# Down projections of an encoder trunk: twelve rows by seven products instead of eight, through a ring of units

## The reference, cut to what matters

```
def swiglu(h, w_gu, w_down):
    u = h @ w_gu
    return (silu(u[..., :D_FF]) * u[..., D_FF:]) @ w_down      # [512, 2816] @ [2816, 1024]

h = h + rmsnorm(swiglu(rmsnorm(h, ffn_pre[l]), ffn_w_gu[l], ffn_w_down[l]), ffn_post[l])    # l = 0, 1
kv = rmsnorm(h, kv_norm) @ w_kv                                # between the two layers
q = rmsnorm(h, mix_pre[1]) @ w_q
```

## Time and profile before

| | |
|---|---|
| median of 3 runs | 1087.94 us |
| the profiled execution's own time | 1087.81 us |
| its span | 1086.0 us |
| TensorE matmul busy | 1076.0 us (99%) |
| VectorE busy | 850.5 us (78%) |
| ScalarE busy | 589.0 us (54%) |
| POOL busy | 27.4 us (3%) |
| granted TensorE clock | 0.999 |

### The profile page before, as it was taken

The page is one execution under the profiler, slowest core; times in us unless marked ns, Lnnn a source line. Parts: engine busy times, 40 slices in busy tenths (PEclk is TensorE's granted clock), DMA queues, the critical chain, the costliest instruction groups (busy, mean ns, idle before and its releaser), DMA issues.

```text
span 1086.0 us, 17578 instructions
## 1 busy us (share of the span) xinstructions
PE 1076.0 (99%) x6925; PEld 967.5 (89%) x6925; DVE 850.5 (78%) x1165; ACT 589.0 (54%) x1013; POOL 27.4 (3%) x40
## 2 busy tenths in 40 slices
PE   8999999999999999999999999999999999999998
PEld 7887787889999999988889888889999999998886
DVE  5878986788888888889857798558988888869834
ACT  6377474565555555556435686555555555555523
POOL 2000000000000000000241000000000000000000
PEclk9999999999999999999999999999999999999999
DMA  6332233332333343251562201141244334341311
GB/s 207 104 102 69 78 108 117 96 98 79 98 116 93 104 117 103 93 194 75 138 175 71 48 1 40 40 117 53 84 118 117 91 105 117 108 151 54 136 58 78
DMA packets 150963, 107.24 MB, mean 99 GB/s; under 512 B 23921, under 2 KB 140769, under 8 KB 150882
## 3 DMA queue, kind: packets, MB, share of 16 engines
q1 hardware_dynamic: 150880, 106.12, 32.3%
q10 hardware_dynamic: 2, 0.00, 0.0%
HBM read 104.01 MB, written 2.10 MB: 98 GB/s over the span
## 4 chain that ended last, share of the span: by engine, by line
PE 96%; ACT 1%; DVE 1%; DMA 1%; issue 0%; DVEq 0%; ACTq 0%
PE ps L2214 12%; PE ps L2212 12%; PE ps L2210 12%; PE ps L1895 8%; PE ps L1896 8%; PE ps L1897 8%; PE ps L1915 8%; PE ps L1917 7%; PE ps L1921 7%; PE ps L1960 2%; PE ps L1962 2%; PE ps L1958 2%; PE ps L2141 1%; PE ps L1928 1%; PE ps L2315 1%; PE ps L2342 1%
## 5 line engine op out<-in xcount | busy, mean ns | idle before, releaser
L2210 PE MATMUL ps<-t_hi,w_hi 128*128 128x256 f32 x608 | 172.1, 283 | 0.0
L2212 PE MATMUL ps<-t_lo,w_hi 128*128 128x256 f32 x608 | 172.1, 283 | 0.0
L2214 PE MATMUL ps<-t_hi,w_lo 128*128 128x256 f32 x608 | 172.1, 283 | 0.0
L1269 DVE TENSOR_TENSOR w_lo<-raw,w_hi 128x1024 fp32r<-128x1024 f32 x81 | 102.1, 1264 | 74.7 <-ACT w_hi L743 74.6
L1895 PE MATMUL ps<-x_hi,w_hi 128*128 128x512 f32 (+1 forms) x384 | 137.5, 358 | 0.0
L1896 PE MATMUL ps<-x_lo,w_hi 128*128 128x512 f32 (+1 forms) x384 | 135.1, 352 | 0.0
L1897 PE MATMUL ps<-x_hi,w_lo 128*128 128x512 f32 (+1 forms) x384 | 135.1, 352 | 0.0
L2214 PE MATMUL ps<-x_hi,w_lo 128*128 128x256 f32 x456 | 129.0, 283 | 0.0
L2212 PE MATMUL ps<-x_lo,w_hi 128*128 128x256 f32 x456 | 129.0, 283 | 0.0
L2210 PE MATMUL ps<-x_hi,w_hi 128*128 128x256 f32 x456 | 129.0, 283 | 0.0
L743 ACT CAST w_hi<-raw 128x1024 fp32r<-128x1024 f32 x82 | 85.4, 1047 | 80.0 <-PE ps L1921 61.5
(11 more groups left out here) (286 smaller groups left out, 2445.9 us busy)
## 6 DMA issues: line engine op xcount, KB each, us to landing
raw<-in_ffn_w_gu SPq DMA_DIRECT2D x88, 512.0 KB, 4.6
raw<-in_ffn_w_down SPq DMA_DIRECT2D x36, 512.0 KB, 4.0
raw<-in_a_w_in SPq DMA_DIRECT2D x24, 512.0 KB, 3.9
raw<-in_a_w_out SPq DMA_DIRECT2D x12, 512.0 KB, 3.5
xr<-in_ffn_w_down SPq DMA_DIRECT2D x8, 512.0 KB, 7.6
raw<-in_b_w_o SPq DMA_DIRECT2D x16, 256.0 KB, 4.0
raw_q<-in_b_w_q SPq DMA_DIRECT2D x12, 256.0 KB, 4.6
h<-in_x SPq DMA_DIRECT2D x4, 512.0 KB, 5.5
```

Of the source, the lines that this page charges most:

```text
L1269: v.tensor_tensor(lo, raw_of(t), hi.bitcast(F32), ALU.subtract).then_inc(w_lo_ready, 1)
L2210: nc.tensor.matmul(ps[:, b, 0:HS], w_hi[:, slot, cols], hi, start=start, stop=False, skip_group_check=True)
L2212: nc.tensor.matmul(ps[:, b, 0:HS], w_hi[:, slot, cols], lo, start=False, stop=False, skip_group_check=True)
L2214: ins = nc.tensor.matmul(ps[:, b, 0:HS], w_lo[:, slot, cols], hi, start=False, stop=j == DC // 2 - 1, skip_group_check=True)
```

## The change: what it does

- The chunk takes twelve rows (4 to 15) instead of eight; the sevenfold scheme stays, each quarter now being six rows deep. Ten rows are plain instead of fourteen.
- Each phase is cut in three units of two rows. Splits, weight sums T1 to T4, matmuls and semaphores go unit by unit (`unit_done` in place of `phase_done`); the token sums S1 to S4 are one instruction each, now 1536 columns.
- The high and low parts of the weights go through a ring: units 0 and 1 of phases 1, 6, 7 and 4 in `x_hi`, their unit 2 in `w_hi` and `w_lo` place 0; phases 2, 3 and 5 in places 1 to 3. Phase 4 runs its units in the order 2, 0, 1.
- The raw weights lie in `raw` (rows 4 to 7), `work` (8, 9), `xr` (10 to 13) and `hr`, in the space of `hid` rows 0 to 3 (14, 15). Rows 8 and 9 are loaded between rows 5 and 6.
- The split of row 16 waits for unit 2 of phase 4; those of rows 17 to 19 for the units of phase 5.
- On VectorE fix_c22 stands before the split of row 16, and fix_c12, fix_c22 follow each other. keep_5 keeps its place on ScalarE.
- The own query tiles are issued later: Q6, Q7 and Q2 behind rows 19, 20 and 21, Q3 behind Q0, Q4 and Q5 behind Q1; each waits for phase 4. POOL scales Q6, Q7, Q2, K, Q0, Q3, V, Q1, Q4, Q5.

```diff
-OWN_LOADS = {15: 6, 16: 7, 17: 2, 18: 3, 19: 4, 20: 5}
+OWN_LOADS = {19: 6, 20: 7, 21: 2}
-C0, CP = 4, 4
+C0, CP = 4, 6
+UNITS = [(q, u) for q in PHASES for u in ((2, 0, 1) if q == 4 else (0, 1, 2))]
...
+        def chunk_b_hi(q, u):
+            if PHASES.index(q) % 2 == 0 and u < 2:
+                return x_hi[:, 4 * u:4 * u + 2, :]
+            return pair_of_weights(w_hi, 1 + u if PHASES.index(q) % 2 else 0)
...
+                def chunk_row(k):
+                    p = k - C0 - 4
+                    if p == 0:
+                        sp.wait_ge(lo_4, SEVEN * (f + 1))
+                    elif p == 2:
+                        sp.wait_ge(p3_done, SEVEN * (f + 1))
+                    elif p == 6:
+                        sp.wait_ge(hidlo_ready, plain_row(f, C0 - 1) + 1)
+                    sp.dma_start(chunk_raw(k), dn_v[f][k]).then_inc(chunk_landed[p], 16)
...
             def load_own_queries(m):
-                if m < 6:
-                    sp.wait_ge(hidlo_ready, plain_row(0, 2 * HID_RING - 1) + 1)
-                else:
+                sp.wait_ge(unit_done, unit(0, 4))
+                if m >= 6:
                     sp.wait_ge(fixes_done, fixed(0, "X"))
...
             load_queries(0)
+            load_own_queries(3)
             chunks(T_V, kv_v[:, :, 1, :])
             load_queries(1)
+            load_own_queries(4)
+            load_own_queries(5)
...
                 elif t >= 4 and chunk_place(t - 4) is not None:
-                    if t % 4 < 2:
-                        act.wait_ge(p7_done_half, 2 * chunk_of(t) + 2)
-                    else:
-                        act.wait_ge(phase_done, finished(chunk_of(t), 5))
+                    f, i = chunk_of(t), t % 4
+                    act.wait_ge(unit_done, unit(f, 4, 2) if i == 0 else unit(f, 5, i - 1))
...
+                chunk_high(5)
+                for t in range(2):
+                    keep_7(t)
+                chunk_high(4)
                 k = C0 + CK
                 split_hi(T_DN[f] + k)
...
+                chunk_low(7)
+                chunk_low(5)
+                chunk_low(4)
                 fix_c12()
+                fix_c22()
                 k = C0 + CK
                 split_lo(T_DN[f] + k)
                 hid_low(k)
                 split_lo(T_DN[f] + k + 1)
-                fix_c22()
                 hid_low(k + 1)
                 fix_c21()
...
+                def unit_by_unit(q):
+                    for at in UNITS:
+                        if at[0] == q:
+                            unit_ready(*at)
+                            for p in range(2):
+                                one(*at, p, 0)
+                                ins = one(*at, p, 1)
+                            ins.then_inc(unit_done, 1)
...
+                for u in range(3):
+                    unit_ready(7, u)
+                    one(7, u, 0, 0)
+                    ins = one(7, u, 1, 0)
+                ins.then_inc(p7_half, 1)
+                for u in range(3):
+                    one(7, u, 0, 1)
+                    one(7, u, 1, 1).then_inc(unit_done, 1)
```

More of the change, by code:

```diff
@@ L100, in raw_before @@
     t -= 4
-    while t >= 0 and (is_gate_tile(t) or own_raw(t) is not None or chunk_place(t) in range(CP, CK)):
+    while t >= 0 and (is_gate_tile(t) or own_raw(t) is not None or chunk_place(t) in range(4, CK)):
         t -= 4
@@ L143, in upto, with unit, summed @@
     return sum(pair_of_seven(i) is None and chunk_place(i) is None for i in range(t + 1))
[L146 to L159, removed]
+def unit(f, q, u=None):
+    return len(UNITS) * f + max(i for i, at in enumerate(UNITS) if at[0] == q and u in (None, at[1])) + 1
+def summed(f, name, u=0):
+    return len(SUMS) * f + SUMS.index((name, u)) + 1
 def fixed(f, name):
@@ L361, in trunk @@
[L361 to L379, removed]
+        def first_rows(u, tok, ring=hid):
+            return ring[:, C0 + 2 * u:C0 + 2 * u + 2, tok]
+        def second_rows(u, tok, ring=hid):
+            return ring[:, C0 + CP + 2 * u:C0 + CP + 2 * u + 2, tok]
@@ new lines, in all_rows, with chunk_raw @@
+        def all_rows(k, tok):
+            return hid[:, k:k + CP, tok]
+        def chunk_raw(k):
+            if k < C0 + 4:
+                return raw[:, (k - C0) % 4, :]
+            return [work[:, 0, :], work[:, 1, :], xr[:, 0, :], xr[:, 1, :], xr[:, 2, :], xr[:, 3, :], hr[:, 0, :],
+                    hr[:, 1, :]][k - C0 - 4]
+        upper = [raw[:, 0:2, :], raw[:, 2:4, :], work[:, :, :]]
+        lower = [xr[:, 0:2, :], xr[:, 2:4, :], hr[:, :, :]]
+        left, right = slice(0, S), slice(S, 2 * S)
@@ new lines, in chunk_b, with chunk_a @@
+        def chunk_b(q, u):
+            tile, cols = {1: (upper, left), 2: (lower, left), 6: (upper, left), 3: (lower, right), 7: (upper, right),
+                          5: (lower, right), 4: (lower, left)}[q]
+            return tile[u][:, :, cols]
+        def chunk_a(q, u):
+            if q == 5:
+                return s1_f[:, 2 * u:2 * u + 2, :]
+            rows, tok = {1: (first_rows, early_tok), 2: (second_rows, early_tok), 6: (first_rows, early_tok),
+                         3: (second_rows, early_tok), 7: (first_rows, late_tok), 4: (second_rows, late_tok)}[q]
+            return rows(u, tok)
@@ L396, in trunk @@
         own_landed = [sem(f"own_landed{i}") for i in range(DC - 2)]
-        xr_landed = [sem(f"xr_landed{p}") for p in range(CP)]
+        chunk_landed = [sem(f"chunk_landed{p}") for p in range(CK - 4)]
         a_high_ready = sem("a_high_ready")
@@ L541, in raw_free @@
                 elif chunk_place(last) is not None:
-                    sp.wait_ge(b_low_ready, phase(chunk_of(last), 7))
+                    sp.wait_ge(b_low_ready, unit(chunk_of(last), 7, chunk_place(last) // 2))
                 else:
@@ L1056, in keep_6 @@
                 def keep_6():
-                    act.wait_ge(phase_done, finished(f, 6))
+                    act.wait_ge(unit_done, unit(f, 6))
                     for t in range(2):
@@ L1650, in chunk_ahead @@
-                    dve.wait_ge(sums_ready, summed(f, "T2"))
-                    dve.wait_ge(b_low_ready, phase(f, 2))
-                    chunk_sum("T4", tb4, b21, tb2, ALU.subtract)
-                    dve.wait_ge(sums_ready, summed(f, "T4"))
+                    chunk_sum(a21, a11, a21, ALU.subtract)
+                    for u in range(3):
+                        chunk_a_low(1, u)
+                    for u in range(3):
+                        chunk_b_low(1, u)
+                    dve.wait_ge(a_low_ready, unit(f, 1))
@@ new lines, in chunk_ahead @@
+                    chunk_sum(a11, s1_f[:, :, :], a11, ALU.subtract)
+                    for u in range(3):
+                        chunk_t3_t2(u)
+                    for u in range(2):
+                        chunk_a_low(2, u)
+                        chunk_b_low(2, u)
+                        chunk_t4(u)
+                    chunk_a_low(2, 2)
+                    dve.wait_ge(sums_ready, summed(f, "S2"))
+                    dve.wait_ge(a_low_ready, unit(f, 2))
+                    chunk_sum(a12, a12, a11, ALU.subtract)
@@ new lines, in one @@
+                def one(q, u, p, t):
+                    tok = slice(t * P, (t + 1) * P)
+                    a_hi, a_lo = chunk_a_hi(q, u)[:, p, tok], chunk_a_lo(q, u)[:, p, tok]
+                    b_hi, b_lo = chunk_b_hi(q, u)[:, p, :], chunk_b_lo(q, u)[:, p, :]
+                    us = [at[1] for at in UNITS if at[0] == q]
+                    into, start, stop = result_of[q][t], q == 1 and u == us[0] and p == 0, u == us[-1] and p == 1
+                    nc.tensor.matmul(into, a_hi, b_hi, start=start, stop=False, skip_group_check=True)
+                    nc.tensor.matmul(into, a_hi, b_lo, start=False, stop=False, skip_group_check=True)
+                    return nc.tensor.matmul(into, a_lo, b_hi, start=False, stop=stop, skip_group_check=True)
@@ L1969, in behind_chunk @@
+                pe.wait_ge(p7_kept, 2 * f + 1)
+                for u in range(3):
+                    unit_ready(5, u)
+                    one(5, u, 0, 0)
+                    one(5, u, 1, 0)
+                pe.wait_ge(p7_kept, 2 * f + 2)
+                for u in range(3):
+                    one(5, u, 0, 1)
+                    one(5, u, 1, 1).then_inc(unit_done, 1)
+                unit_by_unit(4)
             def behind_chunk(f, k, first_tile, hi, lo, k_ready):
```

315 lines of the change are left out of this document (163 added, 152 removed).

## The result

| | median us (lowest to highest, runs) | profiled: span, mean clock | ratio to before, 95% interval |
|---|---|---|---|
| before | 1087.66 (1087.36 to 1087.97, 4) | 1086.0 | |
| changed | 1093.87 (1093.65 to 1095.4, 4) | 1092.0, 0.998 | 1.0060 [1.0043, 1.0077] |

What follows compares the result with a forecast made beforehand. TensorE, busy 1076.0 of 1086.0 us, was taken to bound the kernel. Fewer products (-5.44), chunk-end stalls (+5.2) and the first boundary (+5.2) made +5.0 on 1087.81: 1092.9 us, range 1087.2 to 1096.0.

Steps and rivals of the forecast that it cites:

- TensorE's work: Products for rows 4 to 15: 252 instead of 264 per FFN, saving 5.44 us in both FFNs.
- Inside the chunk: Extra sums and splits during the sevenfold products stay hidden: 0, bounds 0 and 3 us per FFN.
- End of the chunk: Before row 16, TensorE waits on late split, keep_5, fix_c22 and row 16's lows: 2.6 us per FFN, 5.2 both.
- First boundary: Behind the first FFN's chunk, crowded query loads and POOL scalings delay row 21 and the first transpose: 5.2 us, bounds 0 and 8.
- one scaling out: At the first boundary, a landing some tenths away takes one 1.9 us scaling out from before row 21's low: 4.3, not 6.2.
- The rule on SBUF: VectorE instructions with two SBUF inputs and GpSimd ones reading SBUF exclude each other; those with at most one do not contend.
- the other reading: At the first chunk's end, fix_c21 would wait out Q6's scaling, TensorE 0.8 us later at C21; left out of the forecast.
- (a): Rival: only the chunk's end stalls, query scalings find VectorE's gaps; 1087.7 us, no change; chance 0.16.
- (b): Rival: no stall at chunk's end or boundary, keep_5 early enough, loads hidden; full 5.44 gained, 1082.5 us; chance 0.09.
- (c): Rival: no stall at the chunk's end, but crowding behind it takes 5 to 6 us; 1087 to 1089; chance 0.05.
- (d): Rival: VectorE also falls behind inside the chunk, up to 3 us per FFN on top; 1095.9 to 1099; chance 0.07.
- The sum: Whole kernel: -5.44 + 5.2 + 5.2 = +5.0 us, so 1092.9 us; forecast's chance 0.63.

Runs made afterwards that it cites:

- e6: e2 plus Q6 and Q7 loaded earlier, K, Q0, V before Q2 to Q5, and POOL's last six scalings held for normalization steps; 1082.41 us.
- e1: Changed kernel with VectorE making the low parts of row 16 before fix_c22; 1088.83 us.
- e2: Changed kernel with ScalarE doing keep_5 before the split of row 16; 1088.90 us.
- e3: Changed kernel with POOL scaling only one column of eight blocks of each own query tile, all loads and waits kept; 1090.04 us.
- e4: Changed kernel with the own query tiles Q2 to Q7 loaded and scaled behind K, Q0, V and Q1; 1093.36 us.
- e7: e6 with keep_5 back behind the split of row 17, gated scalings kept; 1090.04 us.
- e5: Changed kernel with the edits of e2 and e3 together; 1086.87 us.
- e8: e6 without POOL's six waits, each tile scaled as soon as it has landed; 1084.04 us.

## Why the prediction came out right, step by step

**TensorE's work**, -5.44: shown. In e6, where nothing else is left, the span is 5.4 shorter.

**Inside the chunk**, 0: right. 492.40 to 549.50 is 57.10 us of products without a gap, with VectorE busy 46.9 and ScalarE 32.7 (forecast some 33).

**End of the chunk**, 2.6 each: 2.65 each, and the chain is the one told: keep_5 done at 547.8 (547.42 forecast), the token low some 552.0, TensorE on at 552.16. The forecast times are 0.4 us low because the trace starts later. e1 and e2 show that the chain is the cause. What the step left out is the clock behind the gap: it fell in e3, e4 and e7 (granted clock 0.57 to 0.92 in the windows behind them; in e4 behind the first FFN's alone), not in the profile of the changed kernel.

**First boundary**, 5.2: 4.1 of waits and 1.7 of clock, 5.8. With the clock the size is inside the bounds; the waits alone are a little under the 4.3 to 6.2 laid out, and the near sum owes to the clock, which the forecast had not priced. That part is luck. The split is not the one forecast either: 1.1 before row 21 (4.0 forecast) and 3.0 at the transpose (2.2 forecast). The forecast had row 21's low wait for K's and Q0's scalings; Q7 and Q2 were scaled 0.7 and 0.3 us later than laid out (559.1 for 558.4, 562.3 for 562.0) and the low got in between K's and Q0's, ending at 568.3 for 570.7. That is the case "one scaling out" of the range. The time was kept, not saved: K's and Q0's lows then took 5.64 for two, and the scaled tokens 2.41. The mechanism is shown by e3 (gaps gone with the scalings). What stands behind it, K's place in the DMA queue and with it ScalarE's squares, was in none of the forecast's steps. It had K landing at 563.4, which e5 bears out (563.0), but asked only which operation of VectorE its scaling blocks; it priced ScalarE's squares and root at 1.4 us and did not ask when they could start. In the changed kernel this costs nothing by itself, so the sum did not suffer by it; with the chunk's end mended it is most of the 2.7 us of e5. Mending only what the forecast names, as e5 nearly does, gave 1086.87, not 1082.41.

**The rule on SBUF.** fix_c21, with one operand in PSUM, ran from 553.71 in its usual 1.29, though POOL's scaling, of the usual 1.90, began at 554.37; the next operation, with two SBUF operands, took 2.44. The rule of the Trainium skill (SBUF — State Buffer, "Who interferes with whom") and the trace agree on both halves here, and the 0.8 us of the other reading did not come. The scaled tokens have one SBUF tensor as input and were held up all the same (2.41). By the rule as the prediction tells it they would have passed; the prediction let them wait, and gave no reason. The same section of the Trainium skill makes an exception for faster modes that use both ports, which the prediction left out. The 0.75 us for 1024 columns, where a sum takes 1.22, and the 2.41 beside a scaling agree with it.

**The rivals.** (a) needed the scalings to find VectorE's gaps; they lengthened seven of its operations there. (b) and (c) needed row 16's low by 549.1, it came at 552.0. (d) needed a gap inside the chunk. (b)'s time is that of e6, but only after three edits: keep_5's place, the order of loads and scalings, POOL's waits.

**The sum** was +5.0 for +6.0 in the span. The term that was missing is the fall of the clock, 1.7, with 0.4 of a later start; the gaps alone were 9.4 for 10.4, so two errors of unlike sign met.

## What to carry to other kernels

When an operand's last reader moves to the end of a stage, look at what stands behind the waiting instruction on its queue: here two copies, put ahead of a split that has to wait, were worth 5.0 us in the changed kernel and 7.6 once the boundary was mended. Background work on POOL over SBUF is not free for VectorE: hold it until VectorE has handed on what the critical engine wants, and load first what the other engines' queues wait for. And price a wait of TensorE above its length: with a fall of the clock behind it, 2.65 us cost about 4.

## What was not expected of the hardware

Behind waits of TensorE of 2.1 to 5.4 us the granted clock fell to its lower level (1.2 GHz) for some 3 to 4 us. Each profile's span less e6's 1080.6 and less its gaps leaves 1.0 us (e2), 1.5 (e5, of which 0.4 is a later start of the chunk) and 2.7 for two falls (e7); that is an estimate of what the falls cost. Waits of 1.1 to 1.3 us (before row 21 in the changed kernel, at the second transpose in e8) had none. The falls don't come each time: in the changed kernel's profile the two waits of 2.65 us had none, in e7's both had one. The runs of e5 spread over 4.9 us, those of e6, without a wait, over 1.0; the clock makes a part of this spread. The mean granted clock of e5's fastest run (span 1082.4) is 0.999, of its slowest (1087.3) 0.996, which is some 3.3 us of TensorE's work; but runs with 0.997 lie anywhere from 1083.9 to 1087.0, so the waits must differ too. What decides whether the clock falls is open.
